# A two-part transformer on one core: first products, the attention's end, a border and a bias rearranged

## The reference, cut to what matters

```python
hn = rmsnorm(h, norm_mix_g)                       # block 1
proj = hn @ w_in                                  # 3816 columns: queries, keys, index, latent, gates
merged = sigmoid(g_a) * (o_a @ w_branch_a) + sigmoid(g_b) * (o_b @ w_branch_b)
h = h + merged @ w_out
u = causal_depthwise_conv(rmsnorm(h, norm_ffn_g) @ w_up, conv_w, conv_b)
h = h + (silu(gate) * val) @ w_down
x = rmsnorm(h, norm_final_g)                      # then block 2 starts: y = rms_norm(x, norm_mix[0])
f = lb + (1 - lb) * sigmoid(fz); k = 1 - f        # recurrence, lb from softmax of logits
s_own = q @ k.T * scale + rel_table[t5_bucket(dist)]   # block 3
```

## Time and profile before

| | us |
|---|---|
| median of 3 runs (lowest, highest) | 1031.57 (1031.29, 1032.07) |
| the profiled execution | 1032.62 |
| its span, first to last instruction | 1030.4 |
| PE busy in it | 1002.3 |

### The profile page before, as it was taken

One profiled execution on the slowest core, in us unless ns is written; L12 is line 12 of the kernel. 1 busy time (PEld: TensorE's weight loads), 2 busy tenths in 40 slices (PEclk: granted clock), 3 DMA queues, 4 the chain that ended last, 5 costly groups with the idle time before them and its releaser, 6 DMA issues.

```text
span 1030.4 us, 15777 instructions
## 1 busy us (share of the span) xinstructions
PE 1002.3 (97%) x6433; PEld 860.0 (83%) x6433; DVE 674.6 (65%) x830; ACT 545.6 (53%) x706; POOL 27.1 (3%) x54
## 2 busy tenths in 40 slices
PE   7999999999999997999999999999999999999997
PEld 6888776898888886888789888888899888888885
DVE  5578755678787787968667655556644466555554
ACT  5776554456655665643546454454544546454452
POOL 2120000000000001000000000000000000000000
PEclk9999999999999999999999999999999999999999
DMA  9263333456655644754255655555654247565541
GB/s 298 71 213 116 130 123 127 145 178 204 204 171 195 198 149 148 241 179 154 84 184 184 204 197 176 197 197 174 223 163 143 103 137 243 193 202 174 194 163 41
DMA packets 121708, 175.78 MB, mean 171 GB/s; under 512 B 3040, under 2 KB 90419, under 8 KB 121651
## 3 DMA queue, kind: packets, MB, share of 16 engines
q1 hardware_dynamic: 118844, 168.82, 49.7%
q0 software_dynamic: 1264, 4.18, 1.4%
q10 hardware_dynamic: 1542, 1.96, 0.6%
HBM read 173.89 MB, written 1.06 MB: 170 GB/s over the span
## 4 chain that ended last, share of the span: by engine, by line
PE 87%; DVE 7%; ACT 3%; issue 1%; DMA 1%; POOL 0%; SPq 0%; POOLq 0%; DVEq 0%; ACTq 0%
PE ps L1726 26%; PE ps L1776 22%; PE ps L1747 11%; PE ps L1775 10%; PE ps L1763 4%; PE ps L1790 3%; DVE w_lo L1026 3%; PE ps L1798 2%; PE ps L1778 1%; ACT w_hi L506 1%; PE ps L1840 1%; PE ps L1993 1%; PE ps L2126 1%; PE ps L1979 1%; DMA raw<-in_w_in 1%
## 5 line engine op out<-in xcount | busy, mean ns | idle before, releaser
L1026 DVE TENSOR_TENSOR w_lo<-raw,w_hi 128x2048 fp32r<-128x2048 f32 (+3 forms) x162 | 364.6, 2253 | 134.6 <-ACT w_hi L506 134.3
L1776 PE MATMUL ps<-x_both,w_hi 128*128 128x512 f32 x992 | 342.8, 396 | 1.5 <-DVE w_lo L1026 1.5
L506 ACT ACTIVATE w_hi<-raw 128x2048 fp32r<-128x2048 f32 (+3 forms) x162 | 304.3, 1881 | 62.3 <-PE ps L1726 42.9
L1775 PE MATMUL ps<-x_both,w_lo 128*128 128x256 f32 x868 | 242.0, 279 | 0.0
L1776 PEld LDWEIGHTS ps<-x_both,w_hi 128*128 128x128 f32 x992 | 179.1, 188 | 36.2 <-issue 1.7
L1775 PEld LDWEIGHTS ps<-x_both,w_lo 128*128 128x128 f32 x868 | 163.6, 189 | 5.5
L734 ACT ACTIVATE work<-ps 128x512 f32<-128x512 f32 x66 | 39.3, 596 | 151.8 <-PE ps L1776 135.9
L1726 PE MATMUL ps<-w_hi,x_both 128*128 128x512 f32 (+2 forms) x352 | 111.0, 387 | 0.7 <-ACT work L662 0.5
L1747 PE MATMUL ps<-w_hi,x_both 128*128 128x512 f32 x288 | 96.2, 402 | 2.7 <-DVE x_both L1326 1.9
L1726 PE MATMUL ps<-w_hi,hid_hi 128*128 128x512 f32 x248 | 97.0, 391 | 0.6 <-issue 0.6
L1726 PE MATMUL ps<-w_hi,hid_lo 128*128 128x512 f32 x248 | 96.5, 389 | 0.0
(11 more groups left out here) (258 smaller groups left out, 1236.3 us busy)
## 6 DMA issues: line engine op xcount, KB each, us to landing
raw<-in_ffn_w SPq DMA_DIRECT2D x66, 1024.0 KB, 5.0
raw<-in_w_up SPq DMA_DIRECT2D x22, 1024.0 KB, 5.1
raw<-in_hgrn_w_in SPq DMA_DIRECT2D x16, 1024.0 KB, 5.5
raw<-in_w_in SPq DMA_DIRECT2D x12, 1024.0 KB, 6.5
raw<-in_moba_w_in SPq DMA_DIRECT2D x12, 1024.0 KB, 5.2
raw<-in_w_down SPq DMA_DIRECT2D x11, 1024.0 KB, 5.0
raw<-in_w_out SPq DMA_DIRECT2D x4, 1024.0 KB, 5.1
raw<-in_hgrn_w_out SPq DMA_DIRECT2D x4, 1024.0 KB, 5.7
```

The source lines that it names most:

```text
L506: act.activation(w_hi[:, n % RING, 0:kc * cols], raw[:, n % RING, 0:kc * cols], ACT.Copy).then_inc(s["hi_ready"], 1)
L1026: dve.tensor_tensor(w_lo[:, n % RING, sl], raw[:, n % RING, sl], f32(w_hi[:, n % RING, sl]), ALU.subtract).then_inc(s["lo_ready"], 1)
L1775: pe.matmul(out[:, 0, :], w_lo[:, n % RING, at], x_hi[:, k, :], start=False, stop=False)
L1776: ins = pe.matmul(out, w_hi[:, n % RING, at], x_both[:, k, :, :], start=(k == 0), stop=(k == DC - 1))
```

## The change

1. *Start*: raw x is turned; 1/rms is a scale of the copies out (`copy_proj`, `copy_gate`, now one per token tile). Granule 0 is loaded, rounded and split in two halves; the identity comes by ACT's queue; the low parts of the weights come last in the first two products; taps, bounds and bias row move behind `in_block(1, 0)` on PE and behind `c_scaled` on ACT; the angles stand behind DVE's small variances.
2. *Attention's end*: units 12 to 15 are copied straight to `x_hi` and split one by one; turns move into the tiles of t = 1.
3. *First and last down product* (`first_down_high_first` for block 1, `last_down_high_first` for blocks 1 and 2): parts in another order; the first column half signals by itself.
4. *Recurrence border*: POOL scales the first 512 columns by the gain (`by_gain`), DVE scales and squares the others; POOL scales h and clears buffers; ACT rounds granules nf + 1 and nf + 2 earlier; the bounds are made in units 9 to 12 of the first attention.
5. *Bias*: written 128 times, read back unmirrored, added by DVE in `maxima`; the row lies in `xn`, whose next writer (`gate_branch_a`) waits for the write.

The diff, cut to its core; remarks in parentheses are not code:

```diff
-bias_scratch = nc.dram_tensor("bias_scratch", (HEADS, BIAS_LEN), ...)
+bias_scratch = nc.dram_tensor("bias_scratch", (P, HEADS, BIAS_LEN), ...)
-reverse = const[:, K_REV:K_REV + P]
-bias_row = region(17616, BIAS_LEN, parts=HEADS)
+bias_row = xn[0:HEADS, 1, 0:BIAS_LEN]
@@ sync
-            for n in range(RING):
+            sp.dma_start(dst[:, 0:2, :], first[:, 0:2, c0:c0 + cols]).then_inc(s["first_in"], 16)
+            sp.dma_start(dst[:, 2:4, :], first[:, 2:4, c0:c0 + cols]).then_inc(raw_in[0], 16)
+            for n in range(1, RING):
                 load(n)
@@ gpsimd
-            pool.dma_start(const[:, K_ID:K_ID + P], ...)          (now on act)
+            pool.wait_ge(s["final_in"], 16)
             for t in range(TT):
+                pool.wait_ge(s["h_added"], 5 + 2 * t)
+                pool.tensor_tensor(scaled[:, t, 0:512], h[:, t, 0:512], g_final[:, 0:512], ALU.mult).then_inc(s["by_gain"], 1)
                 power(var[:, 6 + t:7 + t], ...)
...
+            for t in range(TT):
+                pool.wait_ge(s["rstd_ready"], 7 + t)
...
+                pool.tensor_tensor(h[:, t, :], scaled[:, t, :], rstd[:, 4 + t:5 + t].broadcast_to((P, D)), ALU.mult).then_inc(s["h_final"], 1)
+            pool.memset(near.rearrange("p a b -> p (a b)"), 0.0)
+            pool.memset(pairs.rearrange("p a b c -> p (a b c)"), 0.0).then_inc(s["pairs_zero"], 1)
@@ scalar
+            first_operand_hi(0, 2)
+            act.wait_ge(s["first_in"], 16)
+            act.activation(w_hi[:, 0, 0:first_cols], raw[:, 0, 0:first_cols], ACT.Copy).then_inc(s["first_hi"], 1)
+            first_operand_hi(2, 4)
+            act.wait_ge(raw_in[0], 16)
+            act.activation(w_hi[:, 0, first_cols:2 * first_cols], ...).then_inc(s["hi_ready"], 1)
+            first_operand_hi(4, 8)
+            hi_of(1, 2)
             for t in range(TT):                                   (squares of x)
...
-            hi(0)
-            first_operand_hi()
-            hi_of(1, 2)
@@ copy_proj, copy_gate
-                act.activation(proj[:, :, c0:c1], ps[:, bank:bank + 2, 0:c1 - c0], ACT.Copy)
+                act.wait_ge(s["rstd_ready"], 2)
+                for t in range(TT):
+                    ins = act.activation(proj[:, t, c0:c1], ps[:, bank + t, 0:c1 - c0], ACT.Copy, scale=rstd[:, t:t + 1])
@@ taps, bounds and bias row: from behind copy_proj(0) to behind c_scaled, then
-            act.dma_start(bias_scratch, bias_row[:, :])
+            act.dma_start(bias_scratch.rearrange("t h j -> h t j"), bias_row.unsqueeze(1).broadcast_to((HEADS, P, BIAS_LEN)))
-            act.wait_ge(s["bias_out"], 16)                        (ahead of relus(0); now in gate_branch_a)
@@ attention's end, scalar
+                dst = (hid_hi if u < 8 else o_T if u < 12 else x_hi)[:, j, P * t:P * t + P]
+                if u == 12:
+                    act.activation(x_hi[:, 0:2, :], o_T[:, 0:2, :], ACT.Copy).then_inc(s["ohi_ready"], 1)
-            for c in range(0, 4, 2):
-                act.activation(x_hi[:, c:c + 2, :], o_T[:, c:c + 2, :], ACT.Copy).then_inc(s["ohi_ready"], 1)
@@ recurrence border, scalar
             square_both(0)
+            hi(nf + 1)
             for half in range(2):
                 operand_hi(3, 0, half)
-            hi(nf + 1)
+            hi(nf + 2)
             square_both(1)
-            hi(nf + 2)
@@ vector, start
-            normalize(0)
-            lo(0)
-            first_operand_lo()
+            first_operand_lo(0, 4)
+            first_lo(0, s["first_hi"])
+            first_lo(1, s["hi_ready"]).then_inc(s["lo_ready"], 1)
+            first_operand_lo(4, 8)
             lo_of(1, 2)
+            for t in range(TT):
+                variance(0, t)
+            lo(3)
+            (half_rstd, var6, w_idx: now ahead of the angles; the masks go behind lo(4))
@@ vector, attention's end
+                if u == 14:
+                    dve.tensor_tensor(x_lo[:, 0:2, :], o_T[:, 0:2, :], f32(x_hi[:, 0:2, :]), ALU.subtract).then_inc(s["olo_ready"], 1)
+                if u >= 13:
+                    output_lo1(u - 1)
+            units(0, 16, fill_lo, lambda u: gate_branch_b(0) if u == 14 else None)
+            output_lo1(15)
@@ vector, end of the feed-forward block with the conv
                     hidden(10)
+                    post_lo(10)
                     lo(n0 + 32)
-                    post_lo(10)
@@ vector, recurrence border
+            def add_scaled(t):
+                for c in range(2):
+                    down_ready(nf - 1, 4, t, c)
+                    add(t, c, 4 + 2 * c + t)
+                v = scaled[:, t, 512:D]
+                dve.tensor_tensor(v, h[:, t, 512:D], g_final[:, 512:D], ALU.mult).then_inc(s["scaled_done"], 1)
+                dve.scalar_tensor_tensor(squared[:, t, 512:D], v, 1.0, v, ALU.mult, ALU.mult, accum_out=ssq[:, 6 + t:7 + t])
-            (h by rstd, the bounds, both memsets behind lo_of(nf + 1, nf + 2))
@@ vector, maxima of the second attention
+                    then(dve.tensor_tensor(biased, src, bias[:, 2 * j:2 * j + 2, S - n:S], ALU.add))
@@ tensor
-            keep_busy(7, 7)
-            turn_xn()
+            keep_busy(7, 4)
+            turn_x(0)
...
+            first_product(0, 0)
+            first_product(1, 4)
+            in_block(1, 0)
             (taps, bounds, bias row)
             in_block(1, 1)
@@ tensor, branch a and down products
+                pe.wait_ge(s["olo_ready"], 2 if k < 2 else 1 + 2 * t if k == 2 else 4 + t)
+                def first_down_high_first(n):          order (hid_hi, w_hi), (hid_hi, w_lo), (hid_lo, w_hi)
+                def last_down_high_first(p, n):        order (hid_hi, w_hi), (hid_lo, w_hi), (hid_hi, w_lo)
-                down_tile(10, n0 + 32, 0, signals=(3,))
+                last_down_high_first(10, n0 + 32)
                 down_tile(9, n0 + 31, 1)
+                if f == 0:
+                    down_tile(10, n0 + 32, 1, signals=(1,), between={3: [(k_turn + 1, 0, 0)]})
+                    turn_half(k_turn + 1, 0, 1)
@@ tensor, scores2
-                    pe.matmul(dst, qm_T[...], km_T[...], start=True, stop=False)
-                    ins = pe.matmul(dst, reverse, bias[:, head, S - n:S], start=False, stop=True)
+                    ins = pe.matmul(dst, qm_T[...], km_T[...], start=True, stop=True)
```

More of the change, by code:

```diff
@@ L510, in hi_of, with first_operand_hi @@
                     hi(n)
-            def first_operand_hi():
-                for c in range(DC):
+            def first_operand_hi(c0, c1):
+                for c in range(c0, c1):
                     if c % 2 == 0:
@@ L1030, in lo_of, with first_operand_lo @@
                     lo(n)
-            def first_operand_lo():
-                for c in range(DC):
+            def first_operand_lo(c0, c1):
+                for c in range(c0, c1):
                     dve.wait_ge(s["xhi_ready"], 2 * (c // 2) + 2)
@@ L1174, in _ @@
             then(ins)
+            dve.wait_ge(s["posrow_in"], 16)
+            then(dve.tensor_copy(posrow, posrow_i))
+            for t in range(TT):
+                ins = dve.tensor_scalar(see[:, t, :], posrow, pos_col[:, t:t + 1], None, ALU.is_le)
+            then(ins)
+            dve.tensor_scalar(add_b, see, -1.0, UNSEEN, ALU.add, ALU.mult).then_inc(s["masks_ready"], 1)
             lo(5)
@@ L1491, in _ @@
             lo(nf)
-            for c in range(2):
-                add_scaled(0, c)
+            add_scaled(0)
             both_variances(0)
@@ L1497, in _ @@
                 operand_lo(3, 0, half)
-            for c in range(2):
-                add_scaled(1, c)
+            add_scaled(1)
             both_variances(1)
```

310 lines of the change are left out of this document (186 added, 124 removed).

## The result

| | us |
|---|---|
| before, median of 5 runs beside it (lowest, highest) | 1032.07 (1031.29, 1032.70) |
| after, median of 5 runs (lowest, highest) | 1025.54 (1024.86, 1026.71) |
| ratio, with its 95% interval | 0.9939 (0.9925 to 0.9954) |
| forecast | 1015.6, range 1011 to 1021 |

The change is faster by 6.5 us, where 16.0 were forecast; the time lies outside the range. The profiled execution of after took 1024.86, with a span of 1023.0, against a span of 1030.4 before: 7.4 less.

What follows compares the result with a forecast made beforehand. PE, the matmul engine, busy 1002.3 of the 1030.4 us span, was taken as the bound. Six terms summing to 16.0 took the profiled 1032.62 to 1016.6; the median, 1.05 below that execution, gave 1015.6, range 1011 to 1021.

Steps and rivals of the forecast that it cites:

- start: Kernel start: raw x is turned, first product near 10.8 instead of 14.37; 2.25 us lasting at the index turn.
- attention's end, first down product: End of first attention: PE's wait and half clock go, 3.4 us; first down product: its 0.58 wait goes.
- recurrence border: First feed-forward block to recurrence: reordered parts, POOL's help and earlier roundings bring PE to the fourth weights 4.15 us earlier.
- later border: Behind the second feed-forward block: the reordered tile lets DVE add its first half 0.5 earlier, worth 0.46 us.
- bias in the second attention: Second attention: 16 bias matmuls go (5.28 us), DVE adds the bias instead, 0.13 charged; 5.15 us.
- bias write: Writing the bias row to memory 128 times, 1.57 MB in 1024 packets, beside the weights: costed at nothing.
- Costed at nothing: The 128-fold bias write: 64 ns a packet, 4 to 7 us beside the weights, DMA mostly free; no cost.
- The rival that names the write: "Slower than before", chance 0.03: the 128-fold write decides only if it takes over 140 + 16 us; at 200, about 1060.
- from where it was at 409.73 plus half a micro: Recurrence border, second token half: PE goes on at 407.75; the tile that ended at 411.8 ends at 409.2.
- POOL's product might be late: Rival, chance 0.13: POOL's products at the recurrence border take 2.5, the 4.15 shrinks to 2; 1017.8, up to 1020.
- the rule on contention: Recurrence border, POOL's product: the skill adds contention when DVE has two inputs in SBUF; no row isolates it; no size given.
- The clock rival: Chance 0.12: the clock falls in one of the remaining pauses of 0.9 to 1.7 us, 1.53 each time; 1017.1.

Runs made afterwards that it cites:

- e2_one_copy: Kernel after with the bias row written once instead of 128 times, all query rows reading the same one, so each query's own bias is left out: 1017.73 us.
- e5_filler_20: Kernel after with 20 dummy matmuls where PE waits 4.72 us, the write unchanged: 1024.40 us.
- e8_gain_by_dve: Kernel after with 16 bias copies and eight skewed reads, plus POOL's gain products at the recurrence border given back to DVE: 1018.60 us.
- e1: Kernel after with the 128-fold bias write issued later, in unit 2 of the first attention: 1022.56 us.
- e6: Kernel after with 16 copies of the bias row written instead of 128, read by eight DMAs on POOL's queue: 1019.17 us.
- e12: Kernel after with the write's same 1024 packets read from eight partitions four apart (0, 4, 8 to 28), giving another bias: 1018.94 us.
- e13: Kernel after with the write's same 1024 packets read from 16 neighbouring partitions, 64 times each, giving another bias: 1018.76 us.
- e3: Kernel after with 36 dummy matmuls where PE waits 4.72 us, the write unchanged: 1025.66 us.
- e7: Kernel after with the write's same 1024 packets read from 128 partitions, 8 times each, giving another bias: 1018.93 us.
- e10: Kernel after with its bias part undone: row written once, 16 bias matmuls back on PE, DVE's additions gone: 1022.70 us.
- e11: Kernel after, write unchanged, with ACT's rounding and DVE's low part of w_uq put behind the second four relus: 1025.32 us.
- e4: Kernel before with its single bias write made 128-fold, at its place in ACT's stream: 1044.41 us.

## Why the prediction was wrong

What a term was worth is the growth of PE's lead over before, read in e2_one_copy at rows that both kernels have. PE's rows, before and then e2_one_copy; the others of before are in the earlier trace rows:

```profile
72.61 0.50 PE L1726 MATMUL ps<-w_hi,x_both 128*128 128x512 f32 x1 [0.53 <-ACT work L662]
730.68 0.50 PE L1747 MATMUL ps<-w_hi,x_both 128*128 128x512 f32 x1 [0.71 <-DVE w_lo L1026]
835.39 0.66 PE L1840 MATMUL ps<-const,xn 128*128 128x128 f32 x4
```

```profile
70.13 0.50 PE L1787 MATMUL ps<-w_hi,x_both 128*128 128x512 f32 x1 [0.53 <-ACT work L691]
228.94 0.70 PE L2167 MATMUL ps<-w_hi,hid_hi 128*128 128x512 f32 x2
401.97 2.27 PE L1851 MATMUL ps<-x_both,w_hi 128*128 128x256 f32 x16 [0.84 <-DVE x_both L1069]
413.68 0.40 PE L1837 MATMUL ps<-x_both,w_hi 128*128 128x512 f32 x1
720.79 0.50 PE L1808 MATMUL ps<-w_hi,x_both 128*128 128x512 f32 x1 [0.71 <-DVE w_lo L1053]
820.47 0.66 PE L1899 MATMUL ps<-const,xn 128*128 128x128 f32 x4
```

| term | forecast | measured | read between |
|---|---|---|---|
| start | 2.25 | 2.48 | the gate product behind w_uq, 72.61 and 70.13 |
| attention's end, first down product | 3.98 | 3.89 | the first down product, 235.31 and 228.94 (6.37) |
| recurrence border | 4.15 | 3.00 | the first whole granule, 423.05 and 413.68 (9.37) |
| later border | 0.46 | 0.52 | the product behind it, 730.68 and 720.79 (9.89) |
| bias in the second attention | 5.15 | 5.03 | the turn behind it, 835.39 and 820.47 (14.92) |
| bias write | 0 | -7.5 | e2_one_copy against after: 720.79 and 728.28 |
| sum | 16.0 | 7.4 | the spans: 1030.4 - 1023.0 = 7.4 |

**The step that failed** is "Costed at nothing": "64 ns each; so some 4 to 7 us beside the weights, before a stretch where DMA is mostly free. What waits is the first gate of branch a, at about 175". All three parts were wrong. The price per packet came from a queue of other transfers, whose sources are not eight neighbouring partitions; it was 193 ns, and the write lasted 32 us. The stretch was not free: three loads began in it that ACT needed within 20 us. And who waits was sought among those that wait for the write, where the harm went to others, on the same 16 engines: loads from 2.6 to 17.1, ACT's rounding, the relus behind it in order, PE. The rival that names the write asked for over 156 us before it would decide; in truth 32 us were enough, because they need not reach 175 but only meet a load that is needed soon.

On top of the wait came the clock, and a balance at one row gives both: at the gate product after is 7.79 behind e2_one_copy. Of that the longer wait is 64.77 - 60.41 = 4.36; the matmuls between took 13.15 us at half clock, against 9.72 in which 0.53 was a wait, so the clock took 3.96 and the wait of 0.53 was swallowed. The rows of e5_filler_20 show that the clock's part can be had back only in part as long as the loads are late.

**The border** was mis-sized by 1.15. DVE's chain from the first add to the second scaled row did not keep its length, as the prediction said it would: 391.80 to 397.70 before, 385.24 to 391.65 in e2_one_copy, 0.5 longer, and 0.3 longer for the second token half. So the second half's split operand let PE go on at 401.97, which with the lead of 6.37 before the border is 408.34 on the scale of before, where 407.75 was forecast: 0.6. Another 0.6 is a credit of the prediction's own, "from where it was at 409.73 plus half a micro": the rows show no such head start, for the same 16 matmuls follow there in both, 2.04 before (409.73 to 411.77) and 2.11 in e2_one_copy (401.97 to 404.08). Later 0.1 came back. I had weighed that POOL's product might be late; it was not (1.29, forecast 1.4). What I left out is that DVE stands still meanwhile. The prediction said of the rule on contention, in the Trainium skill, GPSIMD Engine Reference, section 8 Key points, that no row isolates it; e8_gain_by_dve beside e2_one_copy now does, at 0.67 us (1.36 with POOL's product, 0.69 without). It does not follow that the 0.6 could be had back: e8, without the overlap, is no earlier, since DVE then has one product more to do.

**The clock rival** (a pause that is left brings the clock down, 0.12, 1.53 us) came true in about half of the profiles: behind the wait of 1.90 at the border the clock fell in e1, e6, e8, e12 and e13, and not in the kernel after, e2, e3, e5, e7, e10 and e11. By their mean clocks it fell in most executions of e6, e7, e8, e12 and e13, at about 2 us each. Two of the five executions of the kernel after had a mean clock of 0.990 where the others had 0.993, and were 1.1 to 1.9 us longer, which fits it; they have no profile. The rival was under-weighted. The argument against it, that the 1.93 of the earlier trace rows had no such stretch in one profile, was one toss of a coin.

**The start** came out near its number (2.48, forecast 2.25; the index turn at 40.53, forecast 41.05), but luck is in it. The prediction let the fourth load land at 22.35; ACT had it at 20.05, 2.3 earlier. The small variances were then done at 26.0 instead of 28.1, and the angles behind them still began at 28.07, where the prediction had them, because they waited for a load of constants that its chain did not have:

```profile
28.07 0.38 DVE L1176 TENSOR_SCALAR ang<-const,stat 128x24 f32<-128x24 f32 x2 [2.01 <-DMA const<-in_const]
```

Two errors of about 2 us cancelled. The wait of 0.8 that PE was to have at the turn did not come: its operand was ready at 40.24, and PE came there at 40.53 by itself. (The sum also starts from 43.3, where the row has 43.38.)

**Right** were the attention's end with its clock, the first down product, the later border, and the second attention, where no wait of PE on DVE is left between the units. The forecast for everything but the write, 1015.6, stands beside 1017.7 for e2_one_copy: 2.1 off. The terms without the write give 14.9 instead of 16.0, nearly all of it the border's 1.15. The rest lies between executions: the forecast put the median 1.05 below the profiled execution, and that of e2_one_copy lies 0.5 above its own (1017.23).

## What to carry to other kernels

A transfer "beside the weights" has a length and a width of its own: work out how long it lasts, here from the partitions that it reads, and ask which loads lie in that time and who waits for them, not only who waits for the transfer. A price per packet holds for transfers of the same shape alone. A standstill of the matmul engine like the 1.90 us here is worth filling with dummy work where nothing shortens it, since the clock may fall behind it; but measure the filler's own length first.

## What the runs showed of the hardware

- 1.57 MB written to memory from 8 neighbouring partitions took 32 us from its issue (48 GB/s), from 16 neighbours 17.4, from 8 partitions four apart about 12, from 128 8.2; the packets alone took 30, 14.5, 8.5 and 4.2, with 6.4, 14.5, 7.5 and 16.9 of them under way at once, at 193, 193, 65 and 64 ns each.
- Such a write on one queue took loads on another from 2.6 to 17.1 us (256 KB) and from 5.2 to 24.5 us (1 MB), though the 16 engines were busy for only 60 to 70% of the time. Per packet the loads took 90 ns beside it, 86 without.
- A DVE product with both inputs in on-chip memory took 1.36 instead of 0.69 while POOL multiplied; the add from PSUM that overlapped POOL's product was not stretched. Beside POOL's two products of 1024 columns (3.89 together) two weight subtractions of DVE took 5.97 (e2_one_copy, from 402.40); before they took 4.48.
- Behind the same wait of about 1.90 us at the border the clock fell to half for 3 to 7 us in some profiles (e1, e6, e8, e12, e13) and not at all in others (after, e2, e3, e5, e7, e10, e11). Within the waits of 4.72 (after) and 5.54 (e11) it fell before PE went on; in e4 it fell 1.8 us behind the end of the wait of 2.54 and was still down behind that of 6.80.
